# State space recurrence: a quarter of the groups moved from VectorE to GpSimd

## The reference, cut to what matters

```
bu   = einsum('blgh,gph->blgp', u, bb)        # complex, as re and im
s[t] = lb * s[t-1] + bu[t]                    # per group and state, complex, over the tokens
y    = Re(einsum('ghp,blgp->blgh', c, s)) + d * u
y    = gelu(y);  val, gate = split(y @ w_glu);  out = val * sigmoid(gate)
```

## Time and profile before

| | us |
|---|---|
| median of 3 runs | 3518.62 |
| lowest, highest | 3517.77, 3519.04 |
| the profiled execution | 3520.24 |
| its span | 3518.4 |
| busy in it: PE, PEld | 3426.6, 2982.6 |
| busy in it: DVE, ACT, POOL | 2285.7, 1792.5, 489.4 |

### The profile page before, as it was taken

How to read it: one execution, slowest core, us unless ns; L and a number is a source line. 1 busy time by engine, 2 the same in 40 slices (tenths; PEclk the granted TensorE clock), 3 DMA queues, 4 the chain that set the end, 5 groups by cost and what they waited for, 6 DMA issues and landing times.

```text
span 3518.4 us, 62869 instructions
## 1 busy us (share of the span) xinstructions
PE 3426.6 (97%) x21968; PEld 2982.6 (85%) x21968; DVE 2285.7 (65%) x3495; ACT 1792.5 (51%) x2753; POOL 489.4 (14%) x538
## 2 busy tenths in 40 slices
PE   9998999999999999999999999999599999999999
PEld 7887888888888888887888888888388888888888
DVE  5786665555555766675766677778955765565565
ACT  5467464545454554553554444444544554454444
POOL 0001310111114100123100001105011000001105
PEclk9999999999999999999999999999899999999999
DMA  6562645555555555553466556667245466555555
GB/s 213 173 186 62 203 153 193 186 192 182 191 186 193 170 188 170 161 172 114 160 192 196 186 189 197 199 221 256 53 131 186 156 191 191 185 185 190 186 186 195
DMA packets 190711, 626.03 MB, mean 178 GB/s; under 512 B 26918, under 2 KB 40424, under 8 KB 190456
## 3 DMA queue, kind: packets, MB, share of 16 engines
q1 hardware_dynamic: 176892, 611.37, 53.9%
q10 hardware_dynamic: 13692, 12.96, 1.3%
HBM read 620.32 MB, written 3.15 MB: 177 GB/s over the span
## 4 chain that ended last, share of the span: by engine, by line
PE 90%; DVE 6%; ACT 2%; DMA 1%; issue 1%; POOL 0%; ACTq 0%; SPq 0%; DVEq 0%; POOLq 0%
PE bank L2094 54%; PE bank L2097 28%; PE m L2062 1%; PE m L2119 1%; DMA w_raw<-stream 1%; DVE prod L1858 1%; DVE w_lo L1162 1%; PE m L2190 1%; PE m L2064 0%; DVE st L1861 0%; DVE st L1863 0%; DVE w_lo L1174 0%; PE m L2121 0%; DVE w_lo L1169 0%; PE m L2071 0%
## 5 line engine op out<-in xcount | busy, mean ns | idle before, releaser
L1162 DVE TENSOR_TENSOR w_lo<-w_raw,w_hi 128x1024 fp32r<-128x1024 f32 x1062 | 1306.2, 1252 | 745.8 <-ACT w_hi L516 739.6
L2094 PE MATMUL bank<-act,w_hi 128*128 128x512 f32 x5920 | 1487.8, 393 | 1.9 <-DVE w_lo L1162 1.2
L516 ACT ACTIVATE w_hi<-w_raw 128x1024 fp32r<-128x1024 f32 x1066 | 1104.3, 1054 | 383.1 <-PE bank L2097 349.9
L2094 PEld LDWEIGHTS bank<-act,w_hi 128*128 128x128 f32 x5920 | 1065.4, 189 | 199.1 <-DVE ev L1178 3.1
L2097 PEld LDWEIGHTS bank<-act,w_lo 128*128 128x128 f32 x5920 | 807.7, 190 | 58.0
L2097 PE MATMUL bank<-act,w_lo 128*128 128x256 f32 x5920 | 825.3, 282 | 0.0
L2094 PE MATMUL bank<-ffn,w_hi 128*128 128x512 f32 x2432 | 613.4, 393 | 2.7 <-DVE w_lo L1174 2.5
L536 ACT ACTIVATE low<-bank 128x256 f32<-128x256 f32 x536 | 205.2, 383 | 739.4 <-PE bank L2097 738.5
L2094 PEld LDWEIGHTS bank<-ffn,w_hi 128*128 128x128 f32 x2432 | 436.2, 189 | 81.8 <-DVE w_lo L1174 3.7
L2097 PEld LDWEIGHTS bank<-ffn,w_lo 128*128 128x128 f32 x2432 | 333.8, 190 | 25.2
L1178 DVE TENSOR_TENSOR ev<-bank,low 128x256 f32<-128x256 f32 x462 | 195.7, 423 | 237.6 <-ACT low L536 234.2
(11 more groups left out here) (444 smaller groups left out, 2373.9 us busy)
## 6 DMA issues: line engine op xcount, KB each, us to landing
w_raw<-stream SPq DMA_DIRECT2D x1148, 512.0 KB, 3.4
b_part<-s_bt ACTq DMA_DIRECT2D x16, 256.0 KB
pow_b<-powers ACTq DMA_DIRECT2D x8, 256.0 KB
pow_b<-powers ACTq DMA_DIRECT2D x16, 128.0 KB
bias<-toeplitz SPq DMA_DIRECT2D x4, 384.0 KB, 8.5
res<-x_t SPq DMA_DIRECT2D x2, 512.0 KB, 8.8
res<-x_t ACTq DMA_DIRECT2D x2, 512.0 KB, 10.8
c_half<-s_c ACTq DMA_DIRECT2D x2, 512.0 KB, 6.1
```

What stands on the lines that cost most here:

```text
L516: a(w_hi[:, q, :], w_raw[:, q, :], ACT.Copy).then_inc(hi_ready, 1)
L1162: e.tensor_tensor(w_lo[:, q, :], w_raw[:, q, :], w_hi[:, q, :].bitcast(F32), ALU.subtract).then_inc(lo_ready, 1)
L2094: mm(bank[w][:, 0:2 * n], w_hi[:, q, wt], x(h * hk + k, 0, 2 * n), start=(h == 0 and k == 0), stop=False)
```

## The change

The scan gets three parts with a count each. Part 0 is the first half (groups 0 to 31) and part 1 the lower half of the second (groups 32 to 47), both on VectorE, in the loop and with the skew of before. Part 2 is groups 48 to 63; GpSimd runs it through all 62 quads, with the same three steps, its instructions having 64, 32 and 32 elements a row. VectorE's for part 1 have the same. GpSimd begins once all tiles of `st` are copied and its own memsets are done. ScalarE's turns of tiles 4 and 5 wait for part 1, of 6 and 7 for part 2. VectorE waits for the end of part 2 too before its last copies. The layout of `st`, `lam` and `prod` stays.

```diff
-    scan_step = [sem(f"scan_step{h}") for h in range(2)]
+    scan_step = [sem(f"scan_step{part}") for part in range(3)]
+    SCAN_GROUPS = (slice(0, 32), slice(32, 48), slice(48, 64))
+    SCAN_IN_HALF = (slice(0, 32), slice(0, 16), slice(16, 32))
+
+    def scan_part(tile):
+        return 0 if tile < 4 else 1 + (tile - 4) // 2
+
+    def scan_operation(e, part, c, step):
+        half, g_ = min(part, 1), SCAN_IN_HALF[part]
+        of = prod[:, half, :, :, g_]
+        now = st[:, c + 1, :, SCAN_GROUPS[part]]
+        if step == 0:
+            wide = [P, 2, 2, g_.stop - g_.start]
+            return e.tensor_tensor(of, lam[:, half, :, :, g_], st[:, c, :, SCAN_GROUPS[part]].unsqueeze(1).to_broadcast(wide), ALU.mult)
+        if step == 1:
+            return e.tensor_tensor(now, now, of[:, 0, :, :], ALU.add)
+        return e.tensor_tensor(now, now, of[:, 1, ::-1, :], ALU.add)
...
             def turn(n, first, end):
-                s.wait_ge(scan_step[n // 4], 3 * (end - 2))
+                s.wait_ge(scan_step[scan_part(n)], 3 * (end - 2))
...
-            def scan(h, c, step):
+            def scan(part, c, step):
 
                 n = 3 * (c - 1) + step
                 if n:
-                    v.wait_ge(scan_step[h], n)
...
+                    v.wait_ge(scan_step[part], n)
+                scan_operation(e, part, c, step).then_inc(scan_step[part], 1)
...
+            v.wait_ge(scan_step[2], 3 * (steps_ - 1))
             v.wait_ge(scan_step[1], 3 * (steps_ - 1))
...
             e.memset(k_rhs[:, :, :], 0.0).then_inc(sem("s5_zero"), 1)
+            g.wait_ge(sem("s5_zero"), 4)
+            g.wait_ge(*inputs_copied(6))
+            g.wait_ge(*inputs_copied(BY_DVE[-1]))
+            g.wait_ge(*inputs_copied(ACT_ORDER[-1]))
+            for c in range(1, QUADS - 1):
+                for step in range(3):
+                    n = 3 * (c - 1) + step
+                    if n:
+                        g.wait_ge(scan_step[2], n)
+                    scan_operation(e, 2, c, step).then_inc(scan_step[2], 1)
             square_sum("post_s5", lambda i, w: None, lambda i, w: (sem("glu_y"), 2 * i + (w + 1)))
```

## The result

The changed kernel takes 3527.76 us (median of 9 runs) against 3517.77 us (median of 9) for the kernel before on the same chips. The ratio is 1.0029 with a 95% interval of 1.0020 to 1.0037: 7 to 13 us slower, 10 us in the middle. One of the nine runs, at a TensorE clock of 0.845, took 3770 us and is not in the ratio.

What follows compares the result with a forecast made beforehand. Taken as the bound: the first half's scan on VectorE, releasing ScalarE, then TensorE. Of two parallel paths, part 0 (+10.8 us) and GpSimd (+8.6), the later gave +11: 3531.2 us profiled, 3529.6 us median; range 3520 to 3562.

Steps and rivals of the forecast that it cites:

- TensorE's clock: TensorE after the scan: states(4,5), if held up, may run at the lower clock; charged nothing, at most 3.5 us.
- The path goes through the first half: Scan's end: part 0's last step releases ScalarE, then TensorE; the second half has 4.1 us of slack.
- GpSimd's small instructions: Part 2's scan: 0.31 us for 64 elements, 0.24 for 32, so 1.03 us a quad undisturbed.
- The 98 ns and the 0.42 us fixed part: Bounds on a GpSimd instruction's fixed cost, giving 0.82 and 1.64 us a quad; 0.17 us was taken.
- The rival with dear instructions: GpSimd's fixed part nearer 0.42 than 0.17 us: +18 to +55 us, 3555 us at 1.6 a quad; chance 0.23.
- One instruction at a time on the shared port: VectorE and GpSimd in the scan: an exclusive lock held for the whole instruction; GpSimd's holds sum to 351 ns.
- Both rivals without hindrance: Scan without collisions: either GpSimd's end decides, 3519.8 us, chance 0.15, or the kernel gains 5 us, 3513.6 us, chance 0.05.
- 1.09 us in step to 1.20 us in series, taken as 1.15: Scan's double quad with collisions, same pace for both engines; from 0.946 us, giving part 0 +10.8 us.
- GpSimd's end is the second clock, 2.2 us behind: GpSimd's end holds VectorE's last copies and so states(4,5): +8.6 us, parallel to part 0's +10.8.
- At most 5.1 us to win: First half's end: VectorE left alone takes about 0.85 us a double quad instead of 0.946, 53 x 0.096 us.
- it does what it says: Rival for the scan: GpSimd's instructions are cheap and pass VectorE unhindered, gaining up to 5 us, 3513.6 us; chance 0.05.
- within: Outcome class for the kernel's time: a change of no more than 0.2%, 7 us; chance 0.22.

Runs made afterwards that it cites:

- e3: Changed kernel with GpSimd's 186 instructions replaced by memsets that read nothing, groups 48 to 63 not carried; ratio 0.9997 to the kernel before.
- e6: Changed kernel plus five 12-quad test stretches behind its last result; both engines together take 0.84 us a quad on VectorE with PSUM, 1.09 all in SBUF.
- e4: Changed kernel with GpSimd's instructions replaced by one-input scratch copies, groups 48 to 63 not carried; one run, 3531.68 us beside 3520.58 of the kernel before.
- e2: Changed kernel with 8 groups on GpSimd instead of 16, VectorE carrying 56; ratio 1.0014 to the kernel before.
- e5: Changed kernel with VectorE carrying all 64 groups again and GpSimd running part 2's shapes into a scratch tile beside it; ratio 1.0040 to the kernel before.
- e8: Changed kernel with 24 groups on GpSimd instead of 16, VectorE carrying 40; ratio 1.0036 to the kernel before.
- e1: Changed kernel with groups 48 to 63 not carried, GpSimd's scan and the waits for it left out; ratio 0.9992 to the kernel before.

## Why the prediction was right, and where it wasn't

The forecast was +11 us, and +10 (7 to 13) was measured. The stage itself shows +8.4 where the sum had 10.8. The 2.4 us too many are 1.6 in the pace of the two engines and 0.8 in TensorE's clock. That the forecast lies within 1 us of the difference of the medians is thus in part luck.

- *The path goes through the first half.* Right: in the changed kernel too part 0's last step releases ScalarE, and that TensorE.
- *GpSimd's small instructions.* Right: 0.31 and 0.24 us worked out, 0.32 and 0.25 measured; 1.03 us a quad against 1.07. The 98 ns and the 0.42 us fixed part were both wrong ends. The rival with dear instructions falls with that.
- *One instruction at a time on the shared port.* Right, and now shown for 0.2 us instructions: e3 (no reads) and e6 (one operand in PSUM) take it away, e4 (one read input) keeps it. The Trainium skill (page SBUF — State Buffer, on the ports that the engines share) says that a VectorE instruction with two SBUF inputs contends with a GpSimd one that reads SBUF, not with one that only writes, and that one with at most one SBUF input, outside the modes that take both ports, doesn't contend. By that, the runs agree: 1.22 us a double quad in e4, 0.855 in e3, 0.84 with the PSUM operand in e6. Both rivals without hindrance fall.
- *1.09 us in step to 1.20 us in series, taken as 1.15.* This was the mis-sized term: the engines do fall in step, and the quad is 1.12 us (1.09 in e6). I had argued that nothing keeps them in step; the collisions themselves do, since whoever is early waits (GpSimd's first add takes 0.31 us beside VectorE and 0.25 alone; in e2 it takes 0.32 and 0.22). The 0.03 us between 1.09 and 1.12 is not explained. The sum for part 0 with 1.12 is 53 x 0.174 = +9.2 us, exactly the table's, so the forecast's 10.8 was 1.6 us high. The same arithmetic gave 1.04, 1.18 and 1.24 for e2, e5 and e8, where 1.025, 1.19 and 1.22 came out.
- *GpSimd's end is the second clock, 2.2 us behind.* Right in kind: the copies behind it were over 1.3 us before TensorE needed them, and in e3 they bind. One sign of being right did not come: VectorE was to be hardly idle ahead of its last copies, and idled 3.01 us.
- *TensorE's clock.* The at most 3.5 us didn't arise, as states(4,5) wasn't held up. Where it was, by 1.83 us in e3, the granted clock was 0.51 for the next 2.5 us, and still the first GLU product came 7.7 us after states(4,5), against 8.0 in the kernel before. What the sum lacked is that the low stretch in states(0,1) and (2,3) can change its length: it became 1.5 us shorter, worth -0.8 us.
- *At most 5.1 us to win, in the rival "it does what it says".* Wrong, and the row was there. VectorE alone gets the 0.855 us, but states(0,1) comes only 1.9 us sooner (e1), as ScalarE's turns had waited just 2.45 us for the scan. I read the releaser off that row and not the length of the wait. The faster case was thus worth 2 to 3 us and could not have been told from no change; its 0.05 belonged to "within".

What stays open: why TensorE's clock rises sooner after the change, which no experiment was aimed at.

No version here beats the kernel before by more than the measurement can tell. With the collision gone, even leaving a quarter of the groups out gives 2.8 us; one that carries them without the collision would need VectorE's factors or products in PSUM, whose eight banks the stage uses for its matrix products. It was not tried in the kernel itself, and with 16 groups it would hardly pay. GpSimd starts 7.57 us after the first scan instruction; 62 quads of 1.06 us and the 0.6 us from its end to states(4,5) seen in e3 put that at 73.9 us by an estimate, 3 us later than before the change. GpSimd's own chain would then be the longest path.

## What to carry to other kernels

Before giving GpSimd a share of a VectorE loop, count the SBUF inputs on both sides: if VectorE's instructions read two and GpSimd's read any, their times on the port add up, on scratch data too (e5); then the share pays only if the holds of GpSimd's instructions are shorter than what VectorE sheds. This is shown for VectorE's tensor_tensor only: the TENSOR_SCALAR of the earlier trace rows reads one tensor of SBUF and was still kept for 4.49 us. Even without a collision, GpSimd's own chain has to end within the slack of what waits for it. Two dependent chains that meet this way fall into step, so their common period can be worked out beforehand from one pair of the one plus one hold of the other, here within 0.03 us. And the gain from a shortened chain ends at the *length* of the wait that it ends, not where the chain itself ends.

## What the runs showed of the hardware

- GpSimd with two inputs, undisturbed and dependent: 0.22 us for 16 elements a row, 0.25 for 32, 0.32 for 64, 0.39 for 96, each 0.08 us behind the one before. Against VectorE (0.186 us at 32 and 0.22 at 64 elements, undisturbed in e1) that is a factor of 1.3 to 1.5; per element, from the difference of the two sizes, it is about 2.1. A scan of short instructions is thus kinder to GpSimd than its rate lets expect.
- A GpSimd memset (0.25 to 0.31 us, 184 and 256 elements) doesn't hinder VectorE instructions with two SBUF inputs: 0.855 us a quad in e3, as in e1.
- VectorE with one operand in PSUM and one in SBUF is as fast in a dependent chain as with both in SBUF, 0.85 us a quad in e6. I had expected it somewhat slower.
